# Second buffers in the attention, the last taps in other banks, squares added in pairs on GpSimd, and eight modulation slices moved behind the convolution

## What is computed

```
m = silu(cond) @ ada_w[l] + ada_b[l]            # 1024 x 6144, six vectors of 1024: shift, scale, gate, twice
h = modulate(rms_norm(x, norm_mix[l]), m[0], m[1])
layer 0: z = h @ ev_w_in                        # latents, queries and keys of 8 attention heads, 4 retention heads
         y = [attention(z), retention(z)] @ ev_w_out
layer 1: a, g = split(h @ od_w_in); u = a * sigmoid(g)
         u = depthwise_conv(u, 31 taps) + b;  u = layer_norm(u);  y = silu(u) @ od_w_out
x = x + m[2] * y
h = modulate(rms_norm(x, norm_ffn[l]), m[3], m[4])
x = x + m[5] * mixture_of_experts(h)            # 32 experts, top 2 of one group, gated MLP of 256
```

## Time and profile before

| | |
|---|---|
| median of 3 executions | 1439.07 us (1438.09 to 1443.93) |
| the profiled execution | 1442.97 us |
| its span in the trace | 1441.1 us |
| TensorE busy | 1260.7 us (87%) |
| VectorE, GpSimd, ScalarE busy | 548.4, 392.4, 376.5 us |
| mean TensorE clock granted | 0.93 of full speed |

### The profile page before, as it was taken

The page is one execution under the profiler, slowest core; times in us unless marked ns, Lnnn a source line. Parts: engine busy times, 40 slices in busy tenths (PEclk is TensorE's granted clock), DMA queues, the critical chain, the costliest instruction groups (busy, mean ns, idle before and its releaser), DMA issues.

```text
span 1441.1 us, 21223 instructions
## 1 busy us (share of the span) xinstructions
PE 1260.7 (87%) x7025; PEld 807.8 (56%) x7026; DVE 548.4 (38%) x1316; ACT 376.5 (26%) x762; POOL 392.4 (27%) x743
## 2 busy tenths in 40 slices
PE   6999998978789859999775889998898689999976
PEld 4666775554457445554442856665675445555436
DVE  2111433675612352222111438998313522222213
ACT  2210145554500311111110245664401311111110
POOL 0200100300000013444334129996000133444430
PEclk9999999879989869999998889999699689999998
DMA  9767645310043148999993931100161379999965
GB/s 383 264 227 275 247 176 228 132 59 1 1 175 120 56 173 314 422 424 422 424 424 125 322 117 59 59 30 1 45 248 59 132 286 396 372 417 422 422 275 223
DMA packets 99943, 322.65 MB, mean 224 GB/s; under 512 B 16181, under 2 KB 49947, under 8 KB 77347
## 3 DMA queue, kind: packets, MB, share of 16 engines
q1 hardware_dynamic: 79280, 288.25, 50.3%
q0 software_dynamic: 12464, 21.91, 4.2%
q10 hardware_dynamic: 8131, 11.57, 2.2%
HBM read 312.41 MB, written 27.08 MB: 236 GB/s over the span
## 4 chain that ended last, share of the span: by engine, by line
PE 65%; DMA 9%; SPq 9%; issue 6%; DVE 6%; POOL 3%; ACT 2%; ACTq 0%; POOLq 0%; DVEq 0%
PE PS L632 10%; PE PS L996 9%; PE PS L1123 9%; PE PS L678 8%; PE PS L1018 5%; SPq L520 5%; DMA ring<-in_moe_w_up 4%; PE PS L1064 3%; SPq L523 3%; PE PS L603 2%; DMA ring<-in_ada_w 2%; PE PS L863 2%; PE PS L981 2%; DVE scratch L1589 2%; DMA arena<-in_moe_w_up 2%
## 5 line engine op out<-in xcount | busy, mean ns | idle before, releaser
L1589 DVE TENSOR_TENSOR arena<-arena,PS 128x128 f32<-128x128 f32 (+3 forms) x109 | 40.2, 386 | 294.7 <-ACT arena L1485 187.7
L632 PE MATMUL PS<-arena,ring 128*128 128x320 f32 x512 | 143.4, 444 | 5.7 <-DVE arena L1879 3.7
L996 PE MATMUL PS<-arena 128*64 128x256 f32 x1152 | 134.0, 383 | 13.0 <-DMA arena<-in_moe_w_up 11.9
L1123 PE MATMUL PS<-arena,ring 128*128 128x320 f32 x512 | 141.8, 438 | 3.5 <-issue 2.2
L678 PE MATMUL PS<-ring,arena 128*128 128x256 f32 (+1 forms) x640 | 142.0, 376 | 1.7 <-ACT arena L1298 1.7
L996 PE MATMUL PS<-ring,arena 128*64 128x256 f32 x1056 | 127.5, 393 | 17.2 <-DMA ring<-in_moe_w_up 15.5
L2365 POOL TENSOR_TENSOR arena<-arena 128x655 f32<-128x655 f32 x91 | 129.8, 1426 | 44.8 <-ACT arena L1556 32.0
L678 PEld LDWEIGHTS PS<-ring,arena 128*128 128x128 f32 x640 | 115.8, 192 | 28.5 <-issue 14.5
L632 PEld LDWEIGHTS PS<-arena,ring 128*128 128x128 f32 x512 | 100.0, 196 | 48.6 <-issue 9.7
L1123 PEld LDWEIGHTS PS<-arena,ring 128*128 128x128 f32 x512 | 97.8, 192 | 47.3 <-issue 8.6
L2134 DVE SCALAR_TENSOR_TENSOR PS<-arena,vecT,PS 128x655 f32<-128x655 f32 x125 | 113.0, 904 | 4.2
(11 more groups left out here) (328 smaller groups left out, 1633.4 us busy)
## 6 DMA issues: line engine op xcount, KB each, us to landing
ring<-in_moe_w_up SPq DMA_DIRECT2D x64, 1024.0 KB
arena<-in_moe_w_up SPq DMA_DIRECT2D x64, 1024.0 KB
ring<-in_ada_w SPq DMA_DIRECT2D x48, 1024.0 KB
ring<-in_moe_w_down SPq DMA_DIRECT2D x32, 1024.0 KB
arena<-in_moe_w_down SPq DMA_DIRECT2D x32, 1024.0 KB
arena<-y_rows ACTq DMA_DIRECT2D x10, 1024.0 KB
ring<-in_od_w_in SPq DMA_DIRECT2D x16, 512.0 KB
ring<-in_ev_w_in SPq DMA_DIRECT2D x7, 1024.0 KB
```

Of the source, the lines that this page charges most:

```text
L632: last = pe.matmul(PS[:, b + n, 0:SEG], w[:, k, c:c + P], src[:, tile(k), n * SEG:(n + 1) * SEG], start=(k == 0), stop=(k == KD - 1))
L996: last = pe.matmul(PS[i * BLK:(i + 1) * BLK, 0, 0:2 * P].rearrange("p (a n) -> p a n", a=2), xblk[:, k, :], w[:, k % 4, :, i * P:(i + 1) * P],
L1123: last = pe.matmul(PS[:, 2 * a + n, 0:SEG], w[:, k, a, :], hT[:, k, n * SEG:(n + 1) * SEG], start=(k == 0), stop=(k == KD - 1))
L1589: return dve.tensor_tensor(out, a, b, op)
```

## The change

Five edits, in the order of the kernel:

1. Slices 40 to 47 of the modulation leave the input projection. They are loaded behind `od_in` and multiplied behind the convolution: four ahead of the sums of squares, four between them. Group 5's copy, transposes, bias and `coef(3)` follow them there. Since the plan loses eight entries ahead of `q_up`, slots shift: `q_up` and `kv_up` lie in slots 3 and 4, `ev_out` in 5, 6, 0, 1; in layer 1 the slices lie in 8, 0 to 6 and `od_out` in 7, 8, 0, 1.
2. The transposed probabilities alternate between banks 4 and 7, and `probT` has a second copy, used by every other group.
3. The values' product always goes to bank 6.
4. The last channel tile gives TensorE 10 taps and VectorE 13, and TensorE's go to banks 0 and 1, without the wait for tile 6.
5. GpSimd adds the squares in pairs, so TensorE sums 4 tiles instead of 8.

```diff
-LAST_TAPS = 9
+LAST_TAPS = 10
 def ada_beside(i):
-    return [] if r == 0 else [8 * g + r - 1] if r < 7 else [8 * g + 6, 8 * g + 7]
+    return [] if r == 0 or g == 5 else [8 * g + r - 1] if r < 7 else [8 * g + 6, 8 * g + 7]
 def weight_plan():
     plan += [("od_in", j) for j in range(8)]
+    plan += [ada(m) for m in range(5 * KD, 6 * KD)]
     plan += [("od_out", j) for j in range(4)]
...
+        def probT(g, hl):
+            return z[:, 0:ST, Z_RQ + 512 * hl:Z_RQ + 512 * (hl + 1)] if g % 2 else late_probT[:, hl, :, :]
+        def turned_prob(n):
+            return quad(4 if n % 2 == 0 else 7)
+        def tap_bank(j):
+            return 0 if j == KD - 1 else 6
# TensorE, project_out
+                    if l == 1 and m == 1:
+                        pe.wait_ge(ev("mod_c"), MODC + 6)
# TensorE, heads
-                if u == 2:
-                    mod_columns(5)
...
-                        pe.wait_ge(ev("mod_c"), MODC + 6)
+                        pe.wait_ge(ev("mod_c"), MODC + 5)
# TensorE, attention
-                    if i >= 3:
-                        pe.wait_ge(ev("pt_a"), i - 2)
-                    if i >= 5:
-                        pe.wait_ge(ev("pt_v"), i - 4)
-                    for j in range(ST + 1 if kind == "lat" else 4):
-                        last = pe.transpose(quad(4 + j // 4)[:, j % 4, :], prob[i % 2][:, j, :], ident)
+                    if i >= 4:
+                        pe.wait_ge(ev("pt_a"), i - 3)
+                    for j in range(4):
+                        last = pe.transpose(turned_prob(i - 2)[:, j, :], prob[i % 2][:, j, :], ident)
+                    if kind == "lat":
+                        if i >= 5:
+                            pe.wait_ge(ev("pt_v"), i - 4)
+                        last = pe.transpose(quad(5)[:, 0, :], prob[i % 2][:, ST, :], ident)
...
-                        pe.wait_ge(ev("o_c"), g - 1)
+                    if g >= 1:
+                        pe.wait_ge(ev("o_c"), g)
# TensorE, convolution
-                else:
+                elif j < KD - 1:
                     pe.wait_ge(ev("conv_v"), conv_ops(j))
...
-            for k in range(KD):
-                pe.wait_ge(ev("ln_sq"), k + 1)
+            pe.wait_ge(ev("conv_v"), conv_ops(KD))
+            for n in range(4):
+                modulation(5 * KD + n)
+            for m in range(KD // 2):
+                pe.wait_ge(ev("conv_p"), adds(KD) + m + 1)
                 for t in range(NT):
...
                 last.then_inc(ev("ln_mm"), 1)
+                modulation(5 * KD + 4 + m)
...
+            mod_columns(5)
             project_out(1, "od_out", cvn, lambda k: k)
# ScalarE: mod_rows(5) moves from the end of the input projection to behind L1565
-                        act.wait_ge(ev("pv_mm"), groups_before(i - 2))
-                        act.activation(probT[h % 2][:, 0:4, t * P:t * P + P], quad(4), ACT.Copy) \
+                        g = 2 + h // 2
+                        act.wait_ge(ev("pv_mm"), g - 1)
+                        act.activation(probT(g, h % 2)[:, :, t * P:t * P + P], turned_prob(i - 2), ACT.Copy) \
# VectorE: mod_bias(5) and coef(3) move into the loop that makes cvn, behind k = 2
# GpSimd, behind the taps
+            for m in range(KD // 2):
+                pool.wait_ge(ev("ln_sq"), 2 * m + 2)
+                pool.tensor_tensor(cv2[:, 2 * m, :], cv2[:, 2 * m, :], cv2[:, 2 * m + 1, :], ALU.add) \
+                    .then_inc(ev("conv_p"), 1)
```

More of the change, by code:

```diff
@@ L246, in build, with probT_ctx @@
         prob = [z[:, :, 0:P], z[:, :, P:2 * P]]
-        probT = [z[:, :, Z_RQ:Z_RQ + 512], z[:, :, Z_RQ + 512:Z_RQ + 1024]]
+        late_probT = front[:, 0:4096].rearrange("p (a j n) -> p a j n", a=2, j=ST)
+        def probT(g, hl):
+            return z[:, 0:ST, Z_RQ + 512 * hl:Z_RQ + 512 * (hl + 1)] if g % 2 else late_probT[:, hl, :, :]
+        def probT_ctx(g, hl):
+            return z[:, ST, Z_RQ + 512 * hl:Z_RQ + 512 * (hl + 1)] if g % 2 else scratch[:, 512 * (1 + hl):512 * (2 + hl)]
+        def turned_prob(n):
+            return quad(4 if n % 2 == 0 else 7)
         oret = z[:, :, Z_RG:Z_RG + 512]
@@ L403, in build @@
             GROUP_END[2 + (hp + 1) * 2 * ST - 1] = 2 + hp
-        def groups_before(i):
-            return i if i < 2 else 2 + (i - 2) // (2 * ST)
         UNITS = [(kind, t) for t in range(NT) for kind in "qk"] + [("k", NT)]
@@ L591, in mod_columns @@
                 for q in range(4):
-                    last = pe.transpose(quad(5 if g == 0 else 7)[:, q, :], mrow[:, q * P:(q + 1) * P], ident)
+                    last = pe.transpose(quad(5 if g == 0 else 7)[:, q, :], (last_mrow if g == 5 else mrow)[:, q * P:(q + 1) * P], ident)
                 last.then_inc(ev("mod_t"), 1)
@@ L888, in _ @@
                             for hl in range(2):
+                                out = PS[hl * VD:(hl + 1) * VD, 6, :]
                                 if g < 2:
                                     h = 4 * g + 2 * pair + hl
-                                    out = PS[hl * VD:(hl + 1) * VD, 6 + g % 2, pair * P:(pair + 1) * P]
-                                    last = pe.matmul(out, vS[:, 5, h, :],
-                                                     probT[0][:, g, (2 * pair + hl) * P:(2 * pair + hl + 1) * P],
+                                    last = pe.matmul(out[:, pair * P:(pair + 1) * P], vS[:, 5, h, :],
+                                                     probT(1, 0)[:, g, (2 * pair + hl) * P:(2 * pair + hl + 1) * P],
                                                      start=True, stop=True)
                                 else:
-                                    last = pe.matmul(PS[hl * VD:(hl + 1) * VD, 6 + g % 2, :],
-                                                     vS[:, j, 2 * (g - 2) + hl, :], probT[hl][:, j, :],
+                                    last = pe.matmul(out, vS[:, j, 2 * (g - 2) + hl, :],
+                                                     probT(g, hl)[:, j, :] if j < ST else probT_ctx(g, hl),
                                                      start=(j == 0), stop=(j == ST))
@@ L1138, in taps @@
                     for n, (c0, c1) in enumerate(((0, HALF), (HALF, SPAN))):
-                        last = pe.matmul(PS[:, 6 + n, 0:c1 - c0], tap_diag(j, w), upad[:, j, w + c0:w + c1],
+                        last = pe.matmul(PS[:, tap_bank(j) + n, 0:c1 - c0], tap_diag(j, w), upad[:, j, w + c0:w + c1],
                                          start=(w == 0), stop=(w == pe_taps(j) - 1))
@@ L1159, in _ @@
                 ln_sums(cv, j, 2, "conv_v", conv_ops(j + 1))
-            for k in range(KD):
-                pe.wait_ge(ev("ln_sq"), k + 1)
+            pe.wait_ge(ev("conv_v"), conv_ops(KD))
[3 more added lines that the diff above has]
+                pe.wait_ge(ev("conv_p"), adds(KD) + m + 1)
                 for t in range(NT):
                     c = t * P if t < ST else CTX0
-                    last = pe.matmul(PS[:, 0, t:t + 1], cv2[:, k, c:c + P], ones[:, 0:1],
-                                     start=(k == 0 and t == 0), stop=(k == KD - 1 and t == NT - 1))
+                    last = pe.matmul(PS[:, 0, t:t + 1], cv2[:, 2 * m, c:c + P], ones[:, 0:1],
+                                     start=(m == 0 and t == 0), stop=(m == KD // 2 - 1 and t == NT - 1))
                 last.then_inc(ev("ln_mm"), 1)
+                modulation(5 * KD + 4 + m)
             pe.wait_ge(ev("diag"), DIAG["ln"] + 1)
@@ L1232, in mod_rows @@
                     act.wait_ge(ev("mod_t"), g)
-                act.activation(mrow, PS[:, 7, :], ACT.Copy).then_inc(ev("mrow_c"), 1)
+                act.activation(last_mrow if g == 5 else mrow, PS[:, 7, :], ACT.Copy).then_inc(ev("mrow_c"), 1)
             def decays():
@@ L1384, in _ @@
             latent_roots(ST)
-            mod_rows(5)
             act.wait_ge(ev("lat_n"), NT)
@@ L1562, in _ @@
                 act.activation(cv2[:, k, :], cv[:, k, :], ACT.Square).then_inc(ev("ln_sq"), 1)
-            act.wait_ge(ev("ln_mm"), 2 * KD)
+            act.wait_ge(ev("ln_mm"), KD + KD // 2)
             act.activation(ss[:, 1, 0:NT], PS[:, 0, 0:NT], ACT.Sqrt, bias=eps, scale=1.0 / CONV) \
                 .then_inc(ev("ln_sq"), 1)
+            mod_rows(5)
             for k in range(KD):
@@ L1842, in _ @@
                         .then_inc(ev("hd_v"), 1)
-            dve.wait_ge(ev("mod_c"), MODC + 6)
+            dve.wait_ge(ev("mod_c"), MODC + 5)
             coef(1)
             coef(2)
-            coef(3)
             for i in range(NATT + 3):
@@ L1850, in _ @@
                     dve.wait_ge(ev("p_t"), i - 2)
[L1851 to L1852 removed]
+                    g = 2 + h // 2
+                    dve.wait_ge(ev("pv_mm"), g - 1)
+                    dve.tensor_copy(probT_ctx(g, h % 2)[:, t * P:t * P + P], quad(5)[:, 0, :]).then_inc(ev("pt_v"), 1)
                 if i < NATT:
@@ L2159, in _ @@
```

(4 more changed lines are left out.)

16 lines of the change are left out of this document (7 added, 9 removed).

## The result

The changed kernel took 1404.1 us (median of 4 runs, 1403.01 to 1407.47), the kernel before on the same chip 1440.93 (4 runs, 1438.09 to 1443.93): ratio 0.974, 95% interval 0.9725 to 0.9755, 36.8 us less (35 to 40 us by the interval). Timed again beside other kernels it took 1402.6 us against 1441.08, ratio 0.9745 (0.9724 to 0.9765). The forecast was 1402.3 us.

What follows compares the result with a forecast made beforehand. TensorE was read as 65% of the chain, weight queue and transfers 18%; the touched stretches were short TensorE waits on one engine. Terms 9.7 + 3.3 + 14.3 + 9.5 = 36.8 us off 1439.07 gave 1402.3 us, range 1392 to 1417.

Steps and rivals of the forecast that it cites:

- rival 2: End of the convolution: clock falls at the first pair and stays; 1407.2 us in all, counted within the forecast's 0.68.
- Two of the signs: End of the convolution: clock of 0.5 through all pairs (wrong); root 8 to 11 us sooner from `taps(6)` (right).
- Front: Input projection: eight slices leave, and the `q_up` wait with its half clock goes; 9.7 us, bounds 7 and 12.
- Heads: Pipeline of units: the 2.90 us wait for group 5's bias and half clock behind it go; 3.3 us, bounds 1.5 and 4.4.
- Attention: Per item, two banks let transposes wait only for their item's scaling; 14.3 us, bounds 8 and 17.2.
- rival 1: Attention gains nothing, two `prob` buffers still limiting it; 1416.6 us, chance 0.15 including half of it.
- The term on idle: Attention: of 15.5 us idle ahead of the transposes, all but 1.2 goes.
- Convolution (a): Last taps: TensorE's 5.77 us wait for VectorE ahead of `taps(7)` goes; channel sums end 5.8 us sooner.
- Convolution (b): Channel sums to end of sums of squares, 17.4 us before: 5.4 us gained warm, -0.6 cold; 3.7 taken.
- Its two cases: Channel sums to end of sums of squares takes 12.0 us at full clock or 18.0 at half.
- (c): Behind the squares: last slice, group copy, transposes, bias and `coef(3)` stay hidden; 0, or 1.5 us lost without cover.
- Rival 4: First experts, both layers: loads wait for the projection to free a slot, fifteen come late; 1477 us, chance 0.02.

Runs made afterwards that it cites:

- `one_bank`: Changed kernel with the turned probabilities transposed and copied through bank 4 alone, second `probT` kept: 1425.3 us, ratio 0.9888.
- `taps_as_before`: Changed kernel with `taps(7)` back on banks 6 and 7, the wait for tile 6's sum, and nine last taps: 1409.48 us, ratio 0.9797.
- `wide_squares`: Changed kernel with pairs of squares summed by multiplying with the full matrix of ones, 328 columns at a time: 1400.9 us, ratio 0.9735.
- `quad_squares`: Changed kernel with all eight slices first and VectorE adding pairs to pairs, so TensorE reads two tiles of squares: 1401.2 us, ratio 0.9705.
- `change_again`: The changed kernel itself, unaltered, timed again beside other kernels: 1402.6 us, ratio 0.9745.
- `squares_single`: Changed kernel without GpSimd's sums of pairs, so TensorE reads eight tiles of squares (80 instructions): 1407.9 us, ratio 0.9786.

## Why the prediction was right, and where its terms were not

The total hit: 36.8 us were summed, and the medians differ by 36.8. That it fits so closely is luck. The terms did not all hit; the attention and what follows it gave more, the squares less, and the errors cancelled. What rival 2 describes came true, a clock that falls behind the first pair and stays low, and its time of 1407.2 us did not, because the other terms made up for it. Two of the signs went against the forecast: three of the four pairs ran at half clock, and the root came 5.9 us sooner counted from `taps(6)`, not 8 to 11.

- **Front, 9.7: measured 10.6**, of which some 0.3 stood in the traces ahead of the front already. The gap of 4.1 us at 226 came as 4.37, with a clock of 0.57 behind it. The mis-sized term is the new cold spell: I took 2.5 us from an old one, and sixteen instructions lost 4.94 - 3.62 = 1.3.
- **Heads, 3.3: measured 3.3.**
- **Attention, 14.3: measured 18.6.** The mechanism was right: `one_bank` shows the idle as the loop through bank 4 (19.4 us), and rival 1 would have left the attention at 105.5 us where it is 86.9. The term on idle was right too: 15.5 - 1.5 = 14.0 us. Two things were left out of the sum. The last product went from 7.34 to 4.51, 2.8 us; I had put it into the bound (17.2) and not into the value, although had the two durations side by side. And an item's own work takes 1.74 us instead of 1.82, which over 32 items would be 2.6 us, more than the 1.8 that remain; both figures come from a few items in the middle, so this part isn't settled to the tenth. Bound and range of this step were too narrow: 18.6 lies above 17.2.
- **Convolution (a), 5.8: measured 5.6** in the ledger, 5.9 by `taps_as_before`.
- **Convolution (b), 3.7: measured 0.3.** This is the step that failed. Its two cases were right: 12.0 us warm and 18.0 cold, and 17.0 came out. Wrong was the choice, "a value between the two", on the ground that slices of 512 columns "kept its clock elsewhere". The clock fell after the first pair and stayed at half through the slices as well, which made them dearer (1.93 us). The earlier trace rows had shown a clock of 0.50 in a fully busy stream of one-column instructions, and that row should have carried the value. `wide_squares` shows it from the other side: same order, nearly the same busy share, the sums as matmuls of 328 columns, and the clock stays at 1.00. The low bound was mis-added too: by the terms of (a) and (b) a cold tail gives 5.8 - 0.6 = 5.2 us, not 4.6, and (a) and (b) together measured 5.9. The Trainium skill ("TensorE: Matmul & The Clock Gate", Part 1) lets the clock go by how busy TensorE has been. If busy is the busy share that the profile shows, the trace does not agree: 12.69 of 13.00 us busy were granted 0.60 with one-column matmuls, 8.90 of 9.00 us 1.00 with 328 columns.
- **(c), 0: right** for the copy, bias and coefficients (the projection began 0.1 us better than the root). "If the clock stays full, 3 us come back in what follows": the slices behind did let TensorE enter the projection at 1.00, and it took 69.16 us instead of 71.31, 2.1 us that my sum did not have.
- **Not in the sum at all:** by the first expert 2.1 us more are gained (32.5 to 34.65); the first `project_out` takes 70.85 us instead of 72.08. About 1.0 of the 2.1 seems to come with the second bank, behind which the attention ends warm: from the end of the last product to the first expert are 132.4 us before, 131.3 in both kernels with one bank, and 130.2 to 130.5 in nine of the ten traces with two (131.2 in `quad_squares`). The rest stays open. Against that stand 1.5 us between the router norm's sums of layer 1 and the last transposes of y, where all traces together spread from 326.2 to 329.5 us (before 326.4, changed 327.9), and 2.3 us at the very end, where the last output lands 6.1 us behind the last y work instead of 3.8. In the other traces that last distance is 3.8 to 5.7, and 3.8 in `change_again`, the same kernel, so it belongs to the execution, not to the change.
- **Rival 4** (first experts late) did not happen. SyncE issued the last load that the projection frees at 450.86, 33.4 us earlier than in the earlier trace rows, nearly the whole shift of the kernel, and the first expert started 53 us behind it:

```profile
450.86 0.43 SPq L538 DMA_DIRECT2D ring<-in_moe_w_down  x1
```

- **Rival 1** did not happen either. The Trainium skill ("TensorE: Matmul & The Clock Gate", HAM oscillation) reports that a second PSUM buffer "gave no further gain" in a matmul kernel. This case does not agree: the second bank alone is 19.4 us of the attention, `one_bank` against the changed kernel, and what it takes away is TensorE's wait of 0.53 us per item for the copy out of the single bank.

## What to carry to other kernels

A double buffer is worth the wait that names it times its count: ask which buffer the waiting instruction needs, and give only that one a twin (bank 7 brought 19 us, `probT` nothing). Where waits get shorter, look at the granted clock of the work right behind them, since time can come back there as well: the last product's 2.8 us were the second largest part of what the sum missed.

A TensorE that the profile shows as busy need not be at full clock: among sums over partitions by one-column matmuls it was granted 0.50 to 0.60, also for the wide work between them, and with the same sums as matmuls of 328 columns 1.00. Before shortening the path to a wait, price what runs behind the wait: three ways to reach the projection 2.9 to 4.7 us sooner kept only 1.4 to 2.3 of it, because they arrived there cold (0.85 to 0.91 granted in its first 16 us).

## What the hardware showed that I had not expected

- Wide slices (512 columns, 32 rows) between one-column groups didn't bring the clock back: they ran at 1.93 us each behind the second, third and fourth pair, while the same eight instructions took 1.06 behind the first. In `squares_single` the granted clock was 0.56 over 23.0 us of unbroken work.
- VectorE's reciprocal costs 4.15 us for 640 columns, 6.5 ns a column, where its product of 128x640 in the changed kernel's diagonals (L1614) takes 0.82. It was the price of keeping the clock in `wide_squares`.
- A sum of two 128x655 tiles in SBUF cost VectorE some 0.85 us twice and 1.63 us once in `quad_squares`, against 1.43 to 1.6 for GpSimd. The slow one began at 980.93, while GpSimd's last sum was running (980.26 to 981.86); the other two ran when GpSimd was done. That the two engines hold each other up here is a guess from this one trace, and no run tests it.
